# A router's fillers, its gate product and one weight load are moved to the start of the experts' stage

## The reference

```python
def grouped_moe(x, w_router, b_router, w_gate, w_up, w_down):
    scores = jax.nn.sigmoid((xt @ w_router).astype(jnp.float32))
    ...
    gates = jnp.sum(jax.nn.one_hot(e_idx, N_EXPERTS, dtype=jnp.float32) * w_sel[..., None], axis=1)
    y = jnp.zeros_like(xt)
    for e in range(N_EXPERTS):
        h = jax.nn.silu(xt @ w_gate[e]) * (xt @ w_up[e])
        y = y + gates[:, e:e + 1] * (h @ w_down[e])
```

## Time and profile before

| | |
|---|---|
| median of 3 runs | 777.86 us (777.48 to 779.97) |
| the profiled execution's own time | 779.4 us |
| its span, first to last instruction | 777.6 us |
| mean granted TensorE clock | 0.987 of full |
| busy: PE, DVE, ACT, POOL | 732.2, 579.5, 482.9, 252.6 us |

### The profile page before, as it was taken

One profiled execution on the slowest core, in us unless ns is written; L12 is line 12 of the kernel. 1 busy time (PEld: TensorE's weight loads), 2 busy tenths in 40 slices (PEclk: granted clock), 3 DMA queues, 4 the chain that ended last, 5 costly groups with the idle time before them and its releaser, 6 DMA issues. The chain is left out here.

```text
span 777.6 us, 12791 instructions
## 1 busy us (share of the span) xinstructions
PE 732.2 (94%) x3881; PEld 603.2 (78%) x3881; DVE 579.5 (75%) x975; ACT 482.9 (62%) x881; POOL 252.6 (32%) x294
## 2 busy tenths in 40 slices
PE   3999999999999899999998899999999999999984
PEld 3898888888888677768786678888888888878862
DVE  6964365556555776685798888888888888889847
ACT  3334355556655665675147368788788888888825
POOL 3132257656664252344411101221222221222111
PEclk9999999999999999999999899999999999999998
DMA  9723311222034853311756759999999999999763
GB/s 342 258 109 129 109 59 44 83 68 68 2 122 143 300 232 121 123 68 45 289 200 270 271 190 383 382 374 381 386 372 372 385 375 374 393 379 389 258 217 162
DMA packets 71485, 179.37 MB, mean 231 GB/s; under 512 B 11687, under 2 KB 28071, under 8 KB 71444
## 3 DMA queue, kind: packets, MB, share of 16 engines
q1 hardware_dynamic: 66692, 166.34, 56.6%
q0 software_dynamic: 4752, 12.51, 6.5%
HBM read 153.20 MB, written 30.42 MB: 236 GB/s over the span
## 5 line engine op out<-in xcount | busy, mean ns | idle before, releaser
L1290 POOL TENSOR_SCALAR me<-me,mrec 128x512 f32<-128x512 f32 (+1 forms) x48 | 65.7, 1370 | 52.2 <-DVE mrec L1469 52.1
L1952 DVE TENSOR_TENSOR eDl<-rawD,eDh 128x1024 fp32r<-128x1024 f32 x68 | 81.2, 1217 | 0.2
L1952 DVE TENSOR_TENSOR eUl<-rawU,eUh 128x1024 fp32r<-128x1024 f32 x68 | 78.8, 1220 | 0.3 <-ACT eUh L1882 0.3
L1952 DVE TENSOR_TENSOR eGl<-rawG,eGh 128x1024 fp32r<-128x1024 f32 x64 | 74.1, 1217 | 1.4 <-ACT eGh L1882 1.4
L2073 POOL DMA_INDIRECT acc_rows<-yg,idx_s x16 | 25.6, 1602 | 134.5 <-ACT yg L1907 134.5
L1882 ACT ACTIVATE eDh<-rawD 128x1024 fp32r<-128x1024 f32 x64 | 64.8, 1053 | 2.4 <-DMA rawD<-in_w_down 2.3
L1882 ACT ACTIVATE eGh<-rawG 128x1024 fp32r<-128x1024 f32 x64 | 62.8, 1052 | 2.1 <-DMA rawG<-in_w_gate 1.9
L1882 ACT ACTIVATE eUh<-rawU 128x1024 fp32r<-128x1024 f32 x64 | 62.3, 1050 | 0.0
L1797 PE MATMUL bank<-eGh,xgT_h 128*128 128x512 f32 x136 | 55.9, 411 | 1.8 <-issue 1.0
L1797 PE MATMUL bank<-eUh,xgT_h 128*128 128x512 f32 x136 | 54.6, 401 | 0.0
L1799 PE MATMUL bank<-eGl,xgT_h 128*128 128x512 f32 x136 | 54.2, 398 | 0.0
(11 more groups left out here) (353 smaller groups left out, 2156.1 us busy)
## 6 DMA issues: line engine op xcount, KB each, us to landing
rawG<-in_w_gate SPq DMA_DIRECT2D x68, 512.0 KB, 9.7
rawU<-in_w_up SPq DMA_DIRECT2D x68, 512.0 KB, 9.5
rawD<-in_w_down SPq DMA_DIRECT2D x68, 512.0 KB, 10.9
wb_raw<-in_w_in SPq DMA_DIRECT2D x8, 512.0 KB, 4.7
wo_raw<-in_w_o SPq DMA_DIRECT2D x8, 512.0 KB, 7.8
xln_rows<-res SPq DMA_DIRECT2D x6, 512.0 KB, 3.8
dqk_high<-st_h SPq DMA_DIRECT2D x8, 384.0 KB, 2.3
dqk_low<-st_l SPq DMA_DIRECT2D x8, 384.0 KB, 3.3
```

Of the source, the lines that this page charges most:

```text
L1290: nc.gpsimd.tensor_scalar(e, e, mrec[:, g % NSB:g % NSB + 1], None, ALU.mult).then_inc(m_p, 1)
L1952: nc.vector.tensor_tensor(wl_[X][i][:], raw_of(X, t, i)[:], f32(wh_[X][i][:]), ALU.subtract).then_inc(s_lo[X], 1)
```

## The change

It gives PE more fillers: 23 instead of 16 before the choices are added up, 23 instead of 18 before the index table, 20 instead of 16 after it, and 3 new ones between turn_x(0) and G(0). It moves PE's gate product from before turn_x(0) to behind U(0), DVE's three `gate_vals` operations to behind the splits of U(0), and the first split of U(0) from before x_low(0) to behind it. SP issues the loads of G(2) only once the first gather has landed. Some router tables change their place in memory, so that they may live longer. `ROUTER_PRODUCTS` is 12, as the number it replaces.

```diff
-    hot = at("hot", 162, [P, 2 * NT, P], BF)
-    in_tile = at("in_tile", 165, [P, 2 * NT, MAX_TILES])
...
+    hot = at("hot", 174, [P, 2 * NT, P], BF)
+    in_tile = at("in_tile", 177, [P, 2 * NT, MAX_TILES])
...
         pe.sem_inc(s_used["D"], used0["D"])
         turn_x(0)
+        keep_busy(3)
         inner("G", 0, range(4))
         turn_x(1)
         inner("U", 0, range(4))
+        pe.wait_ge(s_vals, 2)
+        for n in range(2 * NT):
+            last = nc.tensor.matmul(psum[7][:, 0:3 * MAX_TILES], hot[:, n, :], gate_vals[:, n].rearrange("p a b -> p (a b)"),
+                                    start=(n == 0), stop=(n == 2 * NT - 1))
+        last.then_inc(s_gslots, 1)
         count = iterate(pe, iteration)
...
-        low_part("U", 0, (0,))
         x_low(0, 0)
         x_low(0, 1)
-        low_part("U", 0, (1, 2, 3))
+        low_part("U", 0)
+        gate_values()
         low_part("D", 0)
         low_part("G", 1)
         dve.wait_ge(s_gslots, 1)
...
             sp.wait_ge(s_o, 24)
-            sp.wait_ge(s_log, 2 * NT)
+            sp.wait_ge(s_log, ROUTER_PRODUCTS)
+            sp.wait_ge(s_gather, 16)
             for i in range(4):
                 sp.wait_ge(s_raw["G"][i], 32)
                 sp.dma_start(unit_dst("G", i, 2), unit_src("G", 2, i)).then_inc(s_raw["G"][i], 16)
...
             pe.wait_ge(s_hi["G"], 1)
-            keep_busy(16)
+            keep_busy(23)
             pe.wait_ge(s_member, 1)
...
-            keep_busy(18)
+            keep_busy(23)
             pe.wait_ge(s_vals, 1)
...
-            keep_busy(16)
-            pe.wait_ge(s_vals, 2)
-            for n in range(2 * NT):
-                last = nc.tensor.matmul(psum[7][:, 0:3 * MAX_TILES], hot[:, n, :],
-                                        gate_vals[:, n].rearrange("p a b -> p (a b)"), start=(n == 0), stop=(n == 2 * NT - 1))
-            last.then_inc(s_gslots, 1)
-            experts_pe(pe)
+            keep_busy(20)
+            experts_pe(pe, keep_busy)
...
-            for j in range(3):
-                last = tt(gate_vals[:, :, j, :], in_tile[:], gate_part[:, j, :].unsqueeze(2).to_broadcast(full), ALU.mult)
-            last.then_inc(s_vals, 1)
-            experts_dve(dve)
+
+            def gate_values():
+                for j in range(3):
+                    last = tt(gate_vals[:, :, j, :], in_tile[:], gate_part[:, j, :].unsqueeze(2).to_broadcast(full), ALU.mult)
+                last.then_inc(s_vals, 1)
+
+            experts_dve(dve, gate_values)
```

More of the change, by code:

```diff
@@ L458, in encoder_trunk @@
     idx_f = tmp("idx_f", [P, MAX_TILES])
-    le = at("le", 173.125, [1, MAX_MORE + 1, NE])
+    le = at("le", 172, [1, MAX_MORE + 1, NE])
     te_f = tmp("te_f", [1, MAX_TILES])
-    hot = at("hot", 162, [P, 2 * NT, P], BF)
-    in_tile = at("in_tile", 165, [P, 2 * NT, MAX_TILES])
[L464 to L467, removed]
+    hot = at("hot", 174, [P, 2 * NT, P], BF)
+    in_tile = at("in_tile", 177, [P, 2 * NT, MAX_TILES])
+    vals = at("vals", 178.5, [P, 2 * NT, 2, MAX_TILES], BF)
+    gate_part = at("gate_part", 173, [P, 3, 2 * NT], BF)
+    gate_rest = at("gate_rest", 173.5, [P, 2, 2 * NT])
+    gate_vals = at("gate_vals", 180, [P, 2 * NT, 3, MAX_TILES], BF)
     idx_tab = small("idx_tab", [P, MAX_TILES], I32)
@@ L480, in encoder_trunk @@
     s_part = sem("part_logits_copied")
+    ROUTER_PRODUCTS = 2 * NT
     def parts_done(t):
@@ L1768, in experts_sp, with experts_pe @@
         sp.wait_ge(s_out, 16 * NT)
-    def experts_pe(pe):
+    def experts_pe(pe, keep_busy):
         def xg_chunk(c):
@@ L1946, in experts_act, with experts_dve @@
                                  accum_out=squares2[:, t:t + 1]).then_inc(s_sq2, 1)
-    def experts_dve(dve):
+    def experts_dve(dve, gate_values):
         def low_part(X, t, units=range(4)):
```

## The result

The changed kernel took 781.67 us in the median of 19 runs (779.59 to 784.43), the kernel before 777.59 (776.67 to 780.2): ratio 1.0046, 95% interval 1.0036 to 1.0056. By the ratio it is 3.6 us slower (2.8 to 4.4; the plain medians are 4.1 apart); 781.2 was forecast. The profiled execution's span is 780.3 us and its own time 782.1, 0.4 above its median; the one profiled before lay 1.8 above its own. So the two traces, which differ by 2.7 us in span, need not show all of the 3.6.

The account below looks back on a forecast made before the run. The prediction took PE, 94% busy, to bound the kernel, so a delay of tile 1 delays the end as much. Tile 1 at +0.9 and its slow clock at +2.5 gave +3.4, 781.2 us, range 778.0 to 783.0.

Parts of the forecast that it names:

- The fillers: PE ahead of G(0): more fillers fit the waits and cost nothing as long as the clock holds.
- The first gather: Ahead of G(0): without G(2) loads beside it, it lands 0.1 us sooner, at most some 0.3.
- The second gather: Ahead of turn_x(1): issued at 435.0, beside the moved loads it lands at 440.5, just as PE wants it.
- rival B: Second gather takes 8.3 us, PE waits 2.8 before turn_x(1), clock falls there: +2.8 to +4.5 us; chance 0.10.
- DVE's splits, +0.9: DVE ahead of tile 1: twelve splits and gate_vals in a row start tile 1 at 451.7, 0.9 us later.
- The fall, 2.5: Tile 1 on PE: half clock behind a 3.8 us wait costs 2.5 us, the middle of 1.7 and 3.4.
- The gate product: PE behind U(0): 0.64 us, ends at about 447.9, hidden behind DVE's splits.
- case A: The forecast: tile 1 late by DVE (+0.9), then a clock fall in it (1.7 to 3.4 us); chance 0.52.
- G(0)'s end: Sign on PE: G(0)'s last matmul starts before 441, 2.8 us sooner than before.
- PE's idle time of 3 to 4 us ahead of tile 1: Sign: PE idles 3 to 4 us before tile 1's first matmul at 451.7, the clock at 0.50 after.
- rival D: Loop over tiles: its period stays at 17.9, gaining 5.5 us, less 3.4, for 775.8 us; chance 0.08.
- rival C: No dear fall: clock falls in G(0) as before, or holds through the 3.8 us wait; +0.9, 778.8 us; chance 0.25.

Follow-up runs that it names:

- e3: The kernel before with only the new filler numbers (23, 23, 20 and 3); ratio 0.9995 to the kernel before, -0.4 us.
- e1: The changed kernel with the G(2) loads issued at once, not behind the first gather; ratio 1.0044 to the kernel before, +3.4 us.
- e9: e1 with 16 more fillers on PE behind the gate product, in its wait ahead of tile 1; ratio 1.0019 to the kernel before, +1.5 us.
- e12: e1 with DVE's old order (gate_vals and U(0)'s first split ahead of tile 0's rows); ratio 0.9987 to the kernel before, -1.0 us.
- e7: The changed kernel with the last two of four G(2) loads behind the second gather; ratio 1.0041 to the kernel before, +3.2 us.
- e2: The changed kernel with the G(2) loads behind the second gather, not the first; ratio 1.0039 to the kernel before, +3.0 us.
- e6: The changed kernel with 12 more fillers on PE between G(0) and turn_x(1); ratio 1.0021 to the kernel before, +1.6 us.
- e5: The changed kernel with tile 1's first x_low ahead of gate_tab on DVE; ratio 1.0028 to the kernel before, +2.2 us.
- e4: The kernel before with only the G(2) loads' wait for the first gather added; ratio 0.9992 to the kernel before, -0.6 us.

## Why the prediction was right

**The size and the sign** held: +3.4 forecast, +3.6 (2.8 to 4.4) measured. The way there was another in the profiled execution, so that the number came so close is in part luck, as the end of this section says.

**The fillers** ended where forecast (5.48 us a group, 5.54 forecast), and G(0) ran at full clock, its last matmul before 441. That they cost nothing held in this trace; e3 shows an execution in which they cost 1.9 us.

**The first gather**: a gain of 0.1 forecast; it landed 4.33 us after its issue, 4.42 before. Taking 2 MB out of its way brought nothing that can be seen.

**The second gather** is the term that was mis-sized. I took 5.5 us from its issue to its landing, from how much a scatter is slowed in the loaded loop; it took 8.6, 8.8, 7.7 and 8.4 in the four profiles with 2 MB ahead of it. I had read the loop's 8.3 as time spent behind a scatter; here no scatter was there, and half of the 8.6 was time in which only SP's packets moved. The right bound was the upper one that I had for rival B. I gave B 0.10; the changed kernel's profile and every other one with the full load behind the first gather had its late gather.

**DVE's splits, +0.9**: confirmed by e1 (+1.0), e9 (+0.9) and e12, but in the changed kernel itself they lie hidden behind the late gather.

**The fall, 2.5**: it comes after another wait than forecast, and cost 1.6 in the trace. Behind the wait that was forecast it cost 1.6, 1.6 and 2.8 (e1, e7, e2), and filling a wait gave back 2.0 (e6) and 1.9 (e9). The bounds of 1.7 and 3.4 were about right, and most of the prices lie nearer to the lower one than to my middle.

**The gate product** was to be hidden. Behind a U(0) that ends late it is not: it and gate_tab stand ahead of x_low on DVE, and cost 1.4 (e5). The step that failed is "hidden behind these splits": I took PE's end of the product and did not ask what it would be if U(0) came late. Rival B's 451.9 lies 0.2 above the 451.7 of the splits, without a word on what it is added up from; the trace without the fall's cost comes out there (39.7 - 1.6, 38.1, and 451.9 is 38.0), but the prediction does not name the product as the cause.

So the mechanism of case A is what e1, e2 and e7 run by, and that of B, with the product on top, what the changed kernel ran by. B's price, +2.8 to +4.5, and A's, +2.6 to +4.3, were nearly the same, and that made the number right with the order of the two wrong: luck, as far as the changed kernel's own trace goes. By the prediction's own signs G(0)'s end, the splits without a gap and the loop's period held; PE's idle time of 3 to 4 us ahead of tile 1 did not come (1.36), and the clock stayed at 1.00 behind that wait. That rival D did not happen is shown by the loop's period.

Two small sums of the prediction are off and carry nothing: 440.5 + 1.0 + 5.5 + 0.6 is 447.6 and not 447.9, and in rival C the product would end at 449.39 + 0.23 + 0.64 = 450.3 and not 450.0.

## What to carry to other kernels

An engine that idles ahead of a hand-over is a place to do later work in: moving operations from such idle time to behind the hand-over lengthens the engine's chain by all of them, and the engine that is thereby kept waiting may lose its clock as well. When a load is moved out of one transfer's way, look which transfer it then meets. Where two chains end within a microsecond of each other, price both and the wait that each leaves, and expect no gain from undoing one of them alone.

## What the runs showed of the hardware that was not expected

- A gather of one tile's rows (0.35 MB), issued about 2 us behind the first of four loads of 512 KB, took 7.7 to 8.8 us in four kernels; behind two such loads 4.5; with one or none close ahead 4.1 to 4.5. In the four slow ones its first packet moved 4.3 to 4.5 us behind its issue, in the others 1.7 to 2.0. Nothing between was measured, and why it starts so late was not tried. The Trainium skill (DMA: Bandwidth & Descriptors, Queues, rings and completion order) has the engines take turns between the queues that have work. The traces do not bear that out for the gather's first half, in which 434 packets of SP's queue moved and none of the gather's; in the second half both moved, 394 and 144. Whether the gather had anything queued in the first half no record shows.
- The same program on PE up to the same wait of 1.79 us was followed by half clock in one profiled execution and not in another (e4), which also kept its clock through a wait of 3.01 us. Filled waits raised the mean clock over the runs (0.992 to 0.995 and 0.992 to 0.994, e6 and e9), so waits make falls likelier here, and one execution's trace does not tell whether the next has one.
